# A hybrid decoder layer kernel: masked maxima in one VectorE instruction, values as transposed products, low rank in row groups, state decay off TensorE

## The reference

```
h    = rmsnorm(x) * (1 + scale) + shift
proj = h @ w_in                       # 1024 x 2880
A: sliding-window attention, 8 query heads, 2 kv heads, head_dim 64, window 128,
   in blocks of 128 queries against 256 keys, with a learned sink per head
B: RWKV-7 time mixing, 4 heads x 64 (delta rule with a 64x64 state per head)
C: RG-LRU, width 256, after a causal convolution of width 4
y    = concat(A, B, C) @ w_out        # 1024 x 1024
x    = x + gate * rmsnorm(y)
```

```
s = where(mask, (q . k) / 8, -inf);  m = max(max(s), sink);  p = exp(s - m)
o = (p / (sum(p) + exp(sink - m))) @ v            # then times silu(gate)
a = sigmoid(a0 + ad @ a_up);  w = w0 + tanh(wd) @ w_up      # low rank, 32 + 32 rows
S = S * w + sa (kk * a) + v k                     # per head, a 64x64 state
```

## Time and profile before

| | us |
|---|---|
| median of 3 executions (3137.06 to 3147.09) | 3137.26 |
| the profiled execution | 3135.84 |
| its span in the profile | 3134.1 |
| TensorE busy | 2929.2 |
| VectorE busy | 1724.3 |
| ScalarE busy | 1206.5 |
| GpSimd busy | 115.1 |

### The profile page before, as it was taken

One profiled execution on the slowest core, in us unless ns is written; L12 is line 12 of the kernel. 1 busy time (PEld: TensorE's weight loads), 2 busy tenths in 40 slices (PEclk: granted clock), 3 DMA queues, 4 the chain that ended last, 5 costly groups with the idle time before them and its releaser, 6 DMA issues.

```text
span 3134.1 us, 71117 instructions
## 1 busy us (share of the span) xinstructions
PE 2929.2 (93%) x29140; PEld 2203.2 (70%) x29140; DVE 1724.3 (55%) x4165; ACT 1206.5 (38%) x2739; POOL 115.1 (4%) x229
## 2 busy tenths in 40 slices
PE   4899999999999999999649999999999999999987
PEld 3677777777777777776337777777777777777754
DVE  1565556566656555654415655565556665555544
ACT  0434344434444434443204443344344443334432
POOL 0000000000000000000000000000000000000000
PEclk7999999999999999999759999999999999999996
DMA  9000000000000000000370000000000000000001
GB/s 373 30 22 15 22 22 15 22 22 22 22 15 22 15 22 22 22 9 15 124 295 15 22 15 22 22 22 16 22 22 22 22 16 22 15 22 22 9 15 40
DMA packets 37126, 120.10 MB, mean 38 GB/s; under 512 B 13104, under 2 KB 16304, under 8 KB 36016
## 3 DMA queue, kind: packets, MB, share of 16 engines
q1 hardware_dynamic: 29136, 89.20, 8.0%
q10 hardware_dynamic: 7648, 26.04, 2.1%
HBM read 96.83 MB, written 18.41 MB: 37 GB/s over the span
## 4 chain that ended last, share of the span: by engine, by line
PE 66%; issue 17%; DVE 9%; ACT 3%; DMA 3%; POOL 1%; ACTq 0%; DVEq 0%; POOLq 0%; SPq 0%
PE G L438 15%; PE G L433 13%; PE M L768 8%; PE M L579 4%; PE G L658 4%; PE M L429 3%; PE M L592 2%; DMA RB<-in_w_mod 2%; ACT RA L1026 2%; PE G L444 2%; PE M L433 2%; DVE small L1396 1%; DVE Q L1349 1%; DVE hT L1246 1%; PE M L605 1%
## 5 line engine op out<-in xcount | busy, mean ns | idle before, releaser
L438 PE MATMUL G<-hT,w_in 128*128 128x128 f32 x6144 | 738.2, 278 | 3.4 <-DVE hT L1246 3.4
L438 PEld LDWEIGHTS G<-hT,w_in 128*128 128x128 f32 x6144 | 713.6, 193 | 25.4 <-issue 18.6
L433 PE MATMUL G<-w_in,hT 128*128 128x512 f32 (+1 forms) x1536 | 538.4, 494 | 0.0
L768 PE MATMUL M<-w_out,yT 128*128 128x512 f32 x1024 | 455.3, 598 | 5.2 <-DVE yT L1476 5.2
L768 PEld LDWEIGHTS M<-w_out,yT 128*128 128x128 f32 x1024 | 194.4, 192 | 225.6 <-issue 224.1
L433 PEld LDWEIGHTS G<-w_in,hT 128*128 128x128 f32 x1536 | 236.6, 191 | 159.5 <-issue 152.9
L1349 DVE TENSOR_TENSOR Q<-Q,M 64x256 f32<-64x256 f32 x320 | 133.6, 417 | 118.4 <-PE M L592 115.2
L579 PE MATMUL M<-W 64*64 64x64 f32 x4608 | 162.6, 219 | 6.4 <-issue 6.4
L579 PEld LDWEIGHTS M<-W 64*64 64x64 f32 x4608 | 148.5, 135 | 9.8 <-issue 9.8
L592 PEld LDWEIGHTS M<-Q,W 64*64 64x64 f32 x2560 | 88.2, 134 | 69.3 <-issue 69.3
L991 ACT ACTIVATE W<-M 64x512 f32<-64x512 f32 (+1 forms) x160 | 86.6, 541 | 124.0 <-PE M L579 120.9
(11 more groups left out here) (401 smaller groups left out, 4505.9 us busy)
## 6 DMA issues: line engine op xcount, KB each, us to landing
w_in<-in_w_in SPq DMA_DIRECT2D x2, 11520.0 KB, 32.4
xa<-in_x_prompt SPq DMA_DIRECT2D x16, 512.0 KB, 3.3
RA<-in_w_mod ACTq DMA_DIRECT2D x16, 512.0 KB, 6.7
W<-in_w_mod ACTq DMA_DIRECT2D x16, 512.0 KB, 6.8
w_out<-in_w_out SPq DMA_DIRECT2D x2, 4096.0 KB, 35.5
G<-in_x_prompt SPq DMA_DIRECT2D x16, 512.0 KB, 3.3
x_mid<-RA SPq DMA_DIRECT2D x16, 512.0 KB, 2.6
xa<-x_mid SPq DMA_DIRECT2D x16, 512.0 KB, 3.4
```

What stands on the lines that cost most here:

```text
L433: last = mm(out[:, 0:width], H[:, k, :], Win[:, k, col:col + width], start=k == 0, stop=k == KC - 1)
L438: last = mm(out[0:width, :], Win[:, k, col:col + width], H[:, k, :], start=k == 0, stop=k == KC - 1)
L768: last = mm(o[:, :], yT[:, k, :], Wout[:, k, 512 * h:512 * h + 512], start=k == 0, stop=k == KC - 1)
```

## The change

1. The mask is no longer written by TensorE. `maxima` becomes eight `tensor_tensor_reduce` instructions per tile, each of which reads 256 scores of PSUM per partition, adds the mask, writes the masked scores into `Pm` in SBUF and gives their maximum. `exps` then works in place on `Pm`.
2. VectorE divides the probabilities (`normalise`, two calls per tile on 128x1024) before they are transposed. The division behind `values` goes.
3. `values` has V stationary (64 columns) and the divided probabilities moving (256 columns), four products per call instead of eight, into the upper or lower 64 partitions of G1. The result has channels on partitions, so the transposes of the attention output and ScalarE's copy of them go. The attention gate's projection is made by `channels` (transposed) instead of `fill` for the same reason.
4. The low-rank products take 32 rows each, in row groups 0 and 32, into M0 and M3. The chunk operands are transposed by four 128x128 transposes instead of 16 products of 64x64; ScalarE copies them out in four pieces instead of two.
5. The product of the previous state with the identity goes. GpSimd multiplies the previous state by its decay (`decayed`, 128x128, twice a tile) into a new tile `Sp`, and `state` on VectorE adds: four `scalar_tensor_tensor` of 64x64 per call instead of two `tensor_tensor` of 64x128.
6. `h_hi` moves from VectorE to ScalarE, behind `power(5)`. On TensorE `gates(1)` goes ahead of `next_state(0)`, `probs(0)` behind `outputs(0)`, `values(0)` behind `outputs(1)`. On VectorE the scans of group C go behind the first `rhs`. Both copies of the second transposed probabilities wait for `values(0)`, since `PT` is one buffer.

The core of the diff:

```diff
@@ PE: low rank, chunk transposes, gate projection
-                    for k in range(4):
-                        last = mm(M0[:, P * k:P * k + P], lora[:, P * k:P * k + P], tw[:, :], start=True, stop=True)
+                    for k in range(2):
+                        for r, o in zip((slice(0, LORA), slice(LORA, 2 * LORA)), (M0, M3)):
+                            c = P * k + (0 if o is M0 else 2 * P)
+                            last = mm(o[:, P * k:P * k + P], lora[r, c:c + P], tw[r, :], start=True, stop=True)
...
-                    fill(G1, H, C_GA, 512, range(0, 2))
+                    channels(G1[:, P * 0:P * 1], H, C_GA + P * 0, P)
...
-                        for u in range(U):
-                            for r, m in zip(half, (M3, M4)):
-                                last = mm(m[r, 256 * w + HD * u:256 * w + HD * u + HD], BK[r, w, u, :], ident[r, r],
-                                          start=True, stop=True)
+                        for p in range(PAIRS):
+                            c = 256 * w + P * p
+                            last = T(M3[:, c:c + P], BK[:, w, NCH * p:NCH * p + NCH, :])
@@ PE: scores, values, next_state
-                        for m in (ma, mb):
-                            mm(m[:, :].rearrange("p (c k) -> p c k", c=2), identb[:, :], over(mk[:, :], 1, 2),
-                               start=True, stop=False, skip_group_check=True)
...
-                        for k in range(4):
-                            g = k % 2
-                            for f in range(2):
-                                last = mm(G1[:, HD * (4 * j + k):HD * (4 * j + k) + HD], PT[:, f, k, :],
-                                          Vt[:, f, HD * g:HD * g + HD], start=f == 0, stop=f == 1)
+                        for f in range(2):
+                            for g in range(KV):
+                                r = slice(HD * g, HD * g + HD)
+                                last = mm(G1[r, 256 * j:256 * j + 256], Vt[:, f, r], PT[:, f, g::2, :],
+                                          start=f == 0, stop=f == 1)
...
-                                mm(o[r, c], ident[r, r], prev[r, p, :], start=True, stop=False)
-                            for r, o in zip(half, HB):
-                                mm(o[r, c], bkT[r, 0, u, :], Ub[r, p, :], start=False, stop=False)
+                                mm(o[r, c], bkT[r, 0, u, :], Ub[r, p, :], start=True, stop=False)
@@ DVE
+                    def maxima(j, c, ma, mb):
+                        dve.sem_inc(L["dve_w"], 1)
+                        for g, m in ((0, ma), (1, mb)):
+                            k = 4 * j + 2 * c + g
+                            last = nc.vector.tensor_tensor_reduce(
+                                out=Pm[:, j, 2 * c + g, :], in0=m[:, 256 * c:256 * c + 256], in1=mk[:, :], scale=1.0,
+                                scalar=NEG, op0=ALU.add, op1=ALU.max, accum_out=small[:, 8 + k:9 + k])
+                        return last
...
+                    def normalise(j, ready, done):
+                        dve.wait_ge(ready, DONE(n))
+                        den = small[:, 24 + 4 * j:28 + 4 * j]
+                        link(tt(den, den, small[:, 40 + 4 * j:44 + 4 * j], ALU.add))
+                        link(rcp(den, den))
+                        tt(Pm[:, j], Pm[:, j], over(den, 2, 256), ALU.mult).then_inc(done, 1)
...
+                        for p in range(PAIRS):
+                            for r, o in zip(half, HB):
+                                last = stt(S[r, (m + 1) % 2, p, :], o[r, P + HD * p:P + HD * p + HD], pend[r, p, :],
+                                           Sp[r, m, p, :], ALU.mult, ALU.add)
@@ POOL
+                    def decayed(m):
+                        tt(Sp[:, m], S[:, m % 2], pend[:, :, CH * m + CH - 1:CH * m + CH].to_broadcast([P, PAIRS, HD]),
+                           ALU.mult).then_inc(s["sp_ready"], 1)
```

More of the change, by code:

```diff
@@ L723, in tile @@
                     solve(0)
-                    pe.wait_ge(s["exp0"], DONE(n))
-                    probs(0, M3, M4).then_inc(s["pT0_mm"], 1)
+                    gates(1)
                     next_state(0)
                     outputs(0).then_inc(s["s_mm"], 1)
-                    gates(1)
+                    pe.wait_ge(s["pn0"], DONE(n))
+                    probs(0, M3, M4).then_inc(s["pT0_mm"], 1)
                     pe.wait_ge(s["s_ready"], STEP(n, 1, 2))
                     right_side(1)
+                    gates(2)
+                    solve(1)
+                    pe.wait_ge(s["pn1"], DONE(n))
+                    probs(1, M0, M1).then_inc(s["pT1_mm"], 1)
+                    next_state(1)
+                    outputs(1).then_inc(s["y_mm"], 1)
                     pe.wait_ge(s["pT0_act"], DONE(n))
@@ L733, in tile @@
                     pe.wait_ge(s["ga_copied"], DONE(n))
-                    values(0)
-                    solve(1)
-                    pe.wait_ge(s["exp1"], DONE(n))
-                    probs(1, M0, M1).then_inc(s["pT1_mm"], 1)
-                    next_state(1)
-                    outputs(1).then_inc(s["y_mm"], 1)
-                    gates(2)
+                    values(0).then_inc(s["pv0_mm"], 1)
                     gates(3).then_inc(s["gbc_mm"], 1)
@@ L746, in tile @@
                         fill_rk(n + 1, Hn)
-                    pe.wait_ge(s["yA_tm"], DONE(n))
                     pe.wait_ge(s["yn_ready"], DONE(n))
-                    for k in range(4):
-                        last = T(M4[:, P * k:P * k + P], stA[:, P * k:P * k + P])
-                    last.then_inc(s["yAT_mm"], 1)
+                    pe.sem_inc(L["settled"], 1)
                     for u in range(U):
@@ L923, in h_lo, with h_hi @@
                     last.then_inc(s["hT_lo"], 1)
+                def h_hi(m, H):
+                    act.wait_ge(s["xT_hi"], DONE(m))
+                    for k in range(4, 8):
+                        last = A(H[:, k, :], G0[:, P * (k - 4):P * (k - 4) + P], ACT.Identity, bias=mod[:, k, 0:1],
+                                 scale=gs[:, k, 0:1])
+                    last.then_inc(s["hT_hi"], 1)
                 def copy_rk(m):
@@ L994, in tile @@
                     act.wait_ge(s["btT_mm"], DONE(n))
-                    for r, m in zip(half, (M3, M4)):
-                        last = A(bkT[r], m[r, :].rearrange("p (w u c) -> p w u c", w=2, c=HD), ACT.Copy)
+                    bkm = bkT.rearrange("p w (q m) c -> p (w q) m c", m=NCH)
+                    btm = M3[:, :].rearrange("p (x r c) -> p x r c", r=2, c=HD)
+                    for m in range(NCH):
+                        for r in range(2):
+                            last = A(bkm[half[r], :, m, :], btm[half[m], :, r, :], ACT.Copy)
                     last.then_inc(s["bt_out"], 1)
@@ L1121, in _ @@
             for name in POOL_SEMS:
-                pool.sem_inc(s[name], 1)
+                pool.sem_inc(s[name], TILE_STEPS.get(name, 1))
             tt, ts = nc.gpsimd.tensor_tensor, nc.gpsimd.tensor_scalar
```

108 lines of the change are left out of this document (53 added, 55 removed).

## The result

The changed kernel takes 3032.8 us (3027.81 to 3037.28, 4 executions) against 3137.16 of the kernel before in the same comparison: a ratio of 0.9664 with a 95% interval of 0.9634 to 0.9695. The forecast was 3040. Its profiled span is 3029.6 us, where the old one is 3134.1.

What follows compares the result with a forecast made beforehand. TensorE, busy 85.34 of 86.28 us per tile, was taken as the bound, plus waits its fixed order cannot cover. Work -3.96, old wait -0.69, new waits +1.6 gave -3.05 per tile, -97.6 us over 32: 3040 us, range 3000 to 3110.

Steps and rivals of the forecast that it cites:

- The sum: Per tile, -3.96 of work, -0.69 of old wait and +1.6 of new waits: -3.05 us, times 32 -97.6 us.
- The work: TensorE's work per tile, summed over mask, state, values, gates, transposes and low rank: -3.96 us.
- The waits: Four new TensorE waits per tile, 0.3, 0.9, 0.2 and 0.2: +1.6 us.
- Rival 1: Values and low rank: no overlap in new tile positions, 1.76 per call and 1.16; 54 us, 3094; chance 0.12.
- The estimate of 0.88: One call of values, with 128x64 counted as two independent tiles: 1.76 / 2 = 0.88, 0.26 less than taken.
- The pair of masked maximum and read: VectorE's maximum over 256 elements, 0.42, plus a single-column instruction, between nothing and 0.16: 0.50 us per pair.
- the prediction's own sign: Wrong about waits if VectorE reaches the division over half a microsecond off 1020.7, with scores(0) ending at 1011.5.
- the wait of 0.9 ahead of the first probabilities: TensorE asks for the divided probabilities at 1019.8, VectorE has them at 1020.7: wait 0.9 us per tile.
- rival 2: Masked maximum reads at half speed, 0.77 per pair, +2.16 per tile before the first division: 3109; chance 0.08.
- The other waits: TensorE waits 0.3 at the first right side, 0.2 at the second solve, 0.2 at the next projection.
- rival 3: Slower: VectorE bounds scores to division, 1.0 per pair, tile 0.95 longer, 3168; decides from 0.88; chance 0.06.

Runs made afterwards that it cites:

- the probe: Changed kernel with values(0) putting all four products into the lower half and values(1) taking all 128 columns of V, altering the output: 3061.63 us, one execution.
- the order run: Changed kernel with the loops of values and low rank exchanged, so that neighbouring products share a tile position: 3025.65 us, ratio 0.9652 to the kernel before.
- the run with more maxima: Changed kernel with four more masked-maximum pairs per tile, the first two of each half done twice into scratch: 3069.0 us, ratio 0.9781 to the kernel before.

## Why the prediction was right

- **The sum.** 3.05 us per tile were forecast and 3.39 measured (86.28 to 82.89), 97.6 us and 104.5 of span. The work came out nearly as forecast. The waits were near in sum (1.6 against 1.3) and wrong one by one. From the scores to the next projection 1.88 were forecast; the stretch went from 23.10 (1010.35 to 1033.45) to 20.69 (1060.18 to 1080.87), 2.41. The rest of the tile had 1.17 and gave 0.98.
- **The work.** -3.96 against the rows' -3.71 of busy time. Counted from start to start the four new waits are 1.29 and the old one 0.77, which leaves -3.9 for the work. Values 1.08 per call where 1.14 was taken from `scores`, low rank 0.71 where 0.70, chunk transposes 0.60 where 0.60. The nearest shape in the trace was the right one for the new positions. Rival 1's 1.76 and 1.16 are excluded by these rows, and for values the probe gives the reason, which the order run could not: with one position a call is 1.87, and the choice between 1.14 and 1.76 was the choice between overlap and none. For low rank no run has both products in one row group, so that its gain comes from overlap is not shown. The Trainium skill, page "TensorEngine Tiling (Array Packing)", section "Available Configurations", counts two tiles for 128x64. The estimate of 0.88 from it lies 0.14 under the 1.02 from start to start; the probe (1.87 against 1.02) agrees with two tiles side by side.
- **The pair of masked maximum and read** is the term that was mis-sized: 0.50 was taken for it as 0.42 plus the middle of what a small operation could add. The small one adds nothing, and the large one costs its distance of 0.345 and not its length of 0.42. Eight pairs are 2.76 instead of 4.0. VectorE ends the division 8.2 us behind `scores(0)` (1061.24 to 1069.42) where 9.2 were forecast, so by the prediction's own sign (more than half a microsecond off) it was wrong about the waits. With that the wait of 0.9 ahead of the first probabilities vanishes, as the run with more maxima shows by bringing it back. The half speed of rival 2 did not come: 0.42 per instruction is the rate of a plain one. The rule of the Trainium skill's "Vector Engine (DVE) Microarchitecture Reference", section "Points that are easy to get wrong", would not have it for a PSUM and a bf16 source either. But the Trainium skill states it for the `S2S2D2_STT` instruction shape, and the trace calls the masked maximum CUSTOM_DVE_ANT_0, so that it belongs to that family is the prediction's assumption; no masked maximum here has two float32 SBUF sources.
- **The other waits.** Forecast 0.3, 0.2 and 0.2 at the first right side, the second solve and the next projection; measured 0.21, 0.22 and 0.28. The state was forecast to be just in time with 0.9; four instructions whose start partitions alternate take 1.18, and the wait is 0.35. Together 1.06 in brackets, or 1.29 from start to start, where 1.6 was forecast.
- **Luck.** With the pair at 0.345 and all other terms as they stand, the prediction's own chain loses the 0.9 and the 0.3, and its forecast would have been about 3001 (an estimate from its terms: 4.25 x 32 = 136 us less). The pair's excess of 1.2 us of waits made up for 0.9 that the other waits cost beyond their price. That 3032.8 lies so near 3040 is in part this compensation.
- **A sign that was missed.** The prediction took 1.19 for `scores(0)` from its start to that of `multiply(5)`; in the changed kernel it is 1.06. In the old kernel VectorE's copy of W, which `multiply(5)` reads, ended at 1011.96, 0.10 ahead of it. VectorE's queue was the bound there already:

```profile
1011.53 0.43 DVE L1343 COPY W<-M 64x256 f32<-64x256 f32 x1
```

- **Slower (rival 3)** did not come, since 0.345 per pair is far under its 0.88. Its mechanism decides all the same what the single parts are worth: the mask alone, which the sum priced at 1.04 us of TensorE, made the tile 0.32 longer, and the state's part, priced at 0.51, gave nothing and has the tile 0.12 longer. The sum was right for the whole change and would have been wrong for these parts.

## What to carry to other kernels

When one engine is busy 93% of the span, work taken off it counts only where no second engine's queue ends just behind it; walk both queues from their last common point, and expect a part that is worth nothing alone to pay once the other queue is shortened. Price a new instruction by the start-to-start distance of its neighbours, not by its duration plus that of its helper. After such a change, list the waits that are left and look for work without dependants to put in front of each: here that was worth another 1.3%.

## What the runs showed of the hardware

- `tensor_tensor_reduce` with an accumulator output is two instructions, 0.42 and 0.08 us for 256 elements, and the second is hidden: pairs start every 0.345 us. A plain addition of 256 elements (L1485) is 0.42 long too, and the instruction behind it starts after 0.34 (1085.41 to 1085.75).
- Half-width float32 products in different column positions run beside each other, 1.02 against 1.87 us for four; with runs of two per position the order is indifferent, with runs of four it costs 2.79 against 1.88. In both, the other position's first product starts ahead of three waiting records.
- Four 64x64 operations on VectorE take 1.18 us when the start partition alternates between 0 and 64, and 0.98 when it changes once.
